# Modulation halves in four column quarters of the array, their halves added on GpSimd, their columns turned one stage later

## The reference, cut to what matters

```python
mod = silu(c) @ w_mod + b_mod        # c: 1024 values; w_mod: 1024 x 6144
shift1, scale1, gate1, shift2, scale2, gate2 = split(mod, 6)
h = rmsnorm(x, norm1_g) * (1 + scale1) + shift1
```

## Time and profile before

| what | value |
|---|---|
| median of 3 runs | 1730.06 us (1729.62 to 1731.22) |
| the profiled execution, its time | 1734.61 us |
| its span, first to last instruction | 1732.9 us |
| PE busy | 1720.6 us, 99% |
| DVE busy | 1145.7 us, 66% |
| ACT busy | 861.3 us, 50% |
| POOL busy | 231.0 us, 13% |
| chain that ended last | PE 91%, DVE 4%, DMA 2% |

### The profile page before, as it was taken

The page is one execution under the profiler, slowest core; times in us unless marked ns, Lnnn a source line. Parts: engine busy times, 40 slices in busy tenths (PEclk is TensorE's granted clock), DMA queues, the critical chain, the costliest instruction groups (busy, mean ns, idle before and its releaser), DMA issues.

```text
span 1732.9 us, 31049 instructions
## 1 busy us (share of the span) xinstructions
PE 1720.6 (99%) x12693; PEld 1579.1 (91%) x12693; DVE 1145.7 (66%) x1815; ACT 861.3 (50%) x1412; POOL 231.0 (13%) x291
## 2 busy tenths in 40 slices
PE   9999999999999999999999999999999999999999
PEld 9998798999899879998799998999877888979999
DVE  5774658786667566754677777666665747765553
ACT  5444354674444435443544754454436446555543
POOL 2000042221000000000132212000012515210000
PEclk9999999999999999999999999999999999999999
DMA  8676577445657657765676445777535434466653
GB/s 277 220 246 216 180 244 233 153 144 189 204 192 255 222 171 250 255 209 194 209 234 217 134 160 170 248 238 243 177 118 172 103 93 131 146 194 195 195 189 104
DMA packets 257518, 334.71 MB, mean 193 GB/s; under 512 B 15210, under 2 KB 217168, under 8 KB 257376
## 3 DMA queue, kind: packets, MB, share of 16 engines
q1 hardware_dynamic: 251312, 317.42, 56.4%
q0 software_dynamic: 6064, 15.31, 2.7%
HBM read 327.45 MB, written 1.05 MB: 190 GB/s over the span
## 4 chain that ended last, share of the span: by engine, by line
PE 91%; DVE 4%; DMA 2%; ACT 1%; issue 1%; POOL 0%; SPq 0%; POOLq 0%; DVEq 0%; ACTq 0%
PE bank L757 19%; PE bank L760 19%; PE bank L758 19%; PE bank L801 7%; PE bank L802 7%; PE bank L799 7%; DVE wlo L2013 2%; PE bank L923 1%; ACT whi L1571 1%; DMA mtmp<-mtmp 1%; PE bank L773 1%; PE bank L1049 1%; PE bank L883 1%; PE bank L777 1%; PE bank L781 1%
## 5 line engine op out<-in xcount | busy, mean ns | idle before, releaser
L2013 DVE TENSOR_TENSOR wlo<-raw,whi 128x1024 fp32r<-128x1024 f32 x549 | 669.8, 1228 | 335.3 <-ACT whi L1571 331.2
L1571 ACT ACTIVATE whi<-raw 128x1024 fp32r<-128x1024 f32 x549 | 572.1, 1051 | 405.8 <-PE bank L802 217.3
L757 PE MATMUL bank<-XTh,whi 128*128 128x256 f32 x1984 | 555.6, 280 | 0.0
L760 PE MATMUL bank<-XTh,wlo 128*128 128x256 f32 x1984 | 551.6, 278 | 0.5 <-DVE wlo L2013 0.5
L758 PE MATMUL bank<-XTl,whi 128*128 128x256 f32 x1984 | 551.0, 278 | 0.0
L760 PEld LDWEIGHTS bank<-XTh,wlo 128*128 128x128 f32 x1984 | 374.6, 189 | 1.5 <-DVE wlo L2013 1.4
L757 PEld LDWEIGHTS bank<-XTh,whi 128*128 128x128 f32 x1984 | 372.8, 188 | 2.3
L758 PEld LDWEIGHTS bank<-XTl,whi 128*128 128x128 f32 x1984 | 372.9, 188 | 0.0
L757 PE MATMUL bank<-HCh,whi 128*128 128x256 f32 (+2 forms) x864 | 244.3, 283 | 0.0
L758 PE MATMUL bank<-HCl,whi 128*128 128x256 f32 (+2 forms) x864 | 242.2, 280 | 0.0
L760 PE MATMUL bank<-HCh,wlo 128*128 128x256 f32 (+2 forms) x864 | 242.1, 280 | 0.0
(11 more groups left out here) (370 smaller groups left out, 2367.4 us busy)
## 6 DMA issues: line engine op xcount, KB each, us to landing
raw<-in_ffn_w_dram SPq DMA_DIRECT2D x131, 1024.0 KB, 5.2
raw<-in_w_in_dram SPq DMA_DIRECT2D x76, 1024.0 KB, 5.2
raw<-in_w_mod_dram SPq DMA_DIRECT2D x24, 1024.0 KB, 5.1
raw<-in_w_branch_dram SPq DMA_DIRECT2D x16, 1024.0 KB, 5.0
raw<-in_w_out_dram SPq DMA_DIRECT2D x12, 1024.0 KB, 5.0
raw<-in_w_ffn_gate_dram SPq DMA_DIRECT2D x11, 1024.0 KB, 5.1
raw<-in_w_ffn_up_dram SPq DMA_DIRECT2D x11, 1024.0 KB, 5.1
raw<-in_w_ffn_down_dram SPq DMA_DIRECT2D x8, 1024.0 KB, 5.0
```

Source lines behind the costliest of these rows:

```text
L757: e.matmul(o, hi[:, k, w0:w0 + nc_], xh, start=first and k == 0, stop=False)
L760: m = e.matmul(o, lo[:, k, w0:w0 + nc_], xh, start=False, stop=last and k == nk - 1)
L1571: e.activation(hi_part(n), raw_part(n), ACTF.Copy).then_inc(WHI.did(n), 1)
L2013: e.tensor_tensor(lo_part(n), raw_part(n), hi_part(n).bitcast(F32), ALU.subtract).then_inc(WLO.did(n), 1)
```

## The change

A half is now four matmuls with 32 columns of weights each, one for each block of rows, and each goes to its own 32 partitions of the bank, that is to its own column quarter of the array. The silu values lie in a row of 46, zeros behind them, so that each matmul takes 32 of them of which the first two are the ones wanted. What the other 30 columns yield is not read. The four blocks are not summed in the bank any more. The whole bank is copied to SBUF; the second half goes to a buffer of its own (one of `SUMS`), and GpSimd adds the two (`mod_rows`). Four transposes of 128 x 128 turn the sum, and DVE reduces the four quarters into the columns (`mod_turned`). L919 and `cmb` are gone. The columns of group 1 are made in the next feed-forward part, those of group 2 in the mixer in place of one `settle`, those of groups 7 and 11 where they were. In group 11 the sum of squares stands between the halves instead of inside the first.

```diff
-        csil = sb(ctx, "csil", [128, 8, 2])
+        csil = sb(ctx, "csil", [128, 46])
...
-        cmb = sb(ctx, "cmb", [4, 2])
-        sb(ctx, "gap0", [128, 40])
+        sb(ctx, "gap0", [128, 12])
...
+        def mod_rows_of(g, h):
+            if h == 0 or g == 11:
+                return spare
+            return SUMS[{1: 1, 2: 2, 7: 3}[g]][0]
...
             def modulation_half(g, h, first, last, b):
                 c = w.take_whole()
                 if first:
                     empty(b)
                     q.wait_ge(AMD, ("silu", 1))
-                    if h:
-                        q.wait_ge(AMD, ("row", g, 0))
-                        q.wait_ge(TAB, "cmb")
-                        e.matmul(bank[b][0:2, :], cmb[0:2, :], spare[0:2, :], start=True, stop=False)
                 chunk_here(q, c)
                 for k in range(4):
-                    kk = 4 * h + k
-                    m = e.matmul(bank[b][0:2, :], csil[:, kk, :], raw_whole(c)[:, k, :], start=kk == 0, stop=last and k == 3)
-                    if between and k == 1:
-                        between()
+                    m = e.matmul(bank[b][32 * k:32 * k + 32, :], csil[:, 8 * h + 2 * k:8 * h + 2 * k + 32], raw_whole(c)[:, k, :], start=first, stop=last)
...
             def mod_columns(g, b):
                 q.wait_ge(AMD, ("row", g, 1))
-                q.wait_ge(TAB, "cmb")
+                if g != 11:
+                    q.wait_ge(PLN, ("rows", g))
                 empty(b)
                 for j in range(4):
-                    e.matmul(bank[b][:, 2 * j:2 * j + 2], spare[0:2, j * 128:(j + 1) * 128], cmb[0:2, :], start=True, stop=True)
-                settle(b).then_inc(MOD.did(("columns", g)), 1)
+                    m = e.transpose(bank[b][:, j * 128:(j + 1) * 128], spare[:, j * 128:(j + 1) * 128], ident)
+                m.then_inc(MOD.did(("columns", g)), 1)
...
# tensor: layernorm
-                    if h:
-                        mod_columns(g, row_bank(j))
-                    elif j % 3:
+                    if j % 3:
                         empty(2)
                         settle(2)
# tensor: mixer, behind V
-                empty(3)
-                settle(3)
+                if l:
+                    mod_columns(2, 3)
+                else:
+                    empty(3)
+                    settle(3)
# tensor: second
-                modulation_half(11, 0, True, False, 3, add_squares)
+                modulation_half(11, 0, True, False, 3)
+                add_squares()
                 modulation_half(11, 1, False, True, 3)
# tensor: second feed-forward part of the first layer
+                at = ffn_mods(2 * l + 1)
+                if l == 0:
+                    at[0] = lambda: mod_columns(1, 7)
...
# scalar
-                e.activation(spare[0:2, :], bank[b][0:2, :], ACTF.Copy).then_inc(AMD.did(("row", g, h)), 1)
+                e.activation(mod_rows_of(g, h)[:, :], bank[b][:, :], ACTF.Copy).then_inc(AMD.did(("row", g, h)), 1)
...
# vector
+            def mod_turned(g, b):
+                q.wait_ge(MOD, ("columns", g))
+                parts_of = bank[b][:, :].rearrange("p (a j r) -> p a r j", a=4, j=4)
+                e.tensor_reduce(modc[:, 4 * g:4 * g + 4, :], parts_of[:, :, 0:2, :], AX.X, ALU.add).then_inc(DMD.did(g), 1)
...
# gpsimd
+            def mod_rows(g):
+                q.wait_ge(AMD, ("row", g, 1))
+                e.tensor_tensor(spare[:, :], spare[:, :], mod_rows_of(g, 1)[:, :], ALU.add).then_inc(PLN.did(("rows", g)), 1)
...
             def second():
                 for t in range(2):
                     unit_rows(0, t, 6 + t)
+                mod_rows(7)
                 first_block_gone(q)
...
             for l in range(2):
                 layernorm(3 * l)
+                if l:
+                    mod_rows(2)
                 mixer(l)
                 layernorm(3 * l + 1)
+                if l == 0:
+                    mod_rows(1)
```

More of the change, by code:

```diff
@@ L36 @@
 C_COS, C_SIN, C_FIRST = 384, 640, 896
-C_COSG, C_SING, C_PERMG, C_SCAN, C_GM, C_IN, C_NEG, C_CMB, C_ALL = (
-    896, 1152, 1408, 1536, 2304, 2560, 2816, 3072, 3074)
+C_COSG, C_SING, C_PERMG, C_SCAN, C_GM, C_IN, C_NEG, C_ALL = (
+    896, 1152, 1408, 1536, 2304, 2560, 2816, 3072)
 R_GB, R_DG, R_C, R_CC, R_N1, R_N2, R_BM, R_BA, R_GN, R_NQ, R_NK, R_ALL = (
@@ L578, in lo_part, with csil_of @@
             return wlo[n % 4][:, at:at + a * b].rearrange("p (k c) -> p k c", k=a)
+        def csil_of(k, m):
+            return csil[:, 2 * k + m:2 * k + m + 1]
+        def mod_rows_of(g, h):
+            if h == 0 or g == 11:
+                return spare
+            return SUMS[{1: 1, 2: 2, 7: 3}[g]][0]
         def raw_whole(c):
@@ L908, in modulation, with modulation_half @@
                 emptied[b] = ((DMD, g),)
-            def modulation_half(g, h, first, last, b, between=None):
+            def modulation_half(g, h, first, last, b):
                 c = w.take_whole()
@@ L1557, in tensor @@
                 layernorm(3 * l + 1)
-                ffn_up(2 * l + 1, xt, x_ready(3 * l + 2), ffn_mods(2 * l + 1))
+                at = ffn_mods(2 * l + 1)
+                if l == 0:
+                    at[0] = lambda: mod_columns(1, 7)
+                ffn_up(2 * l + 1, xt, x_ready(3 * l + 2), at)
                 ffn_down(2 * l + 1, context() if l else None)
@@ L1583, in mod_row @@
                 q.wait_ge(MOD, ("mod", g, h))
-                if g in ROW_BEFORE:
-                    q.wait_ge(MOD, ("columns", ROW_BEFORE[g]))
-                e.activation(spare[0:2, :], bank[b][0:2, :], ACTF.Copy).then_inc(AMD.did(("row", g, h)), 1)
+                if h == 0 or g == 11:
+                    if g in ROW_BEFORE:
+                        q.wait_ge(MOD, ("columns", ROW_BEFORE[g]))
+                e.activation(mod_rows_of(g, h)[:, :], bank[b][:, :], ACTF.Copy).then_inc(AMD.did(("row", g, h)), 1)
             def ffn_up(i, at):
@@ L1612, in silu_c @@
                 q.wait_ge(AMD, "cols")
+                q.wait_ge(PST, "sel")
+                pairs = csil[:, 0:16].rearrange("p (k m) -> p k m", m=2)
                 for j, r in enumerate((R_C, R_CC)):
-                    e.activation(csil[:, :, j], cols[:, r:r + 8], ACTF.Silu).then_inc(AMD.did(("silu", j)), 1)
+                    e.activation(pairs[:, :, j], cols[:, r:r + 8], ACTF.Silu).then_inc(AMD.did(("silu", j)), 1)
             def ffn_mods(i):
@@ L2021, in sum_up @@
                     q.wait_ge(MOD, ("columns", BEFORE[g]))
+                if (g, h) == (3, 0):
+                    q.wait_ge(PLN, ("rows", 1))
                 for k in (2 * step, 2 * step + 1):
@@ L2025, in sum_up @@
                         if kk == 0:
-                            e.tensor_scalar(acc[:, :], raw_whole(c)[:, k, :], csil[:, kk, m:m + 1], None, ALU.mult).then_inc(
+                            e.tensor_scalar(acc[:, :], raw_whole(c)[:, k, :], csil_of(kk, m), None, ALU.mult).then_inc(
                                 DMD.did(("sum", g, m, kk), ("whole", c), ("sums", g)), 1)
@@ L2029, in sum_up @@
                             q.wait_ge(DMD, ("sum", g, m, kk - 1))
-                            e.scalar_tensor_tensor(acc[:, :], raw_whole(c)[:, k, :], csil[:, kk, m:m + 1], acc[:, :], ALU.mult, ALU.add).then_inc(
+                            e.scalar_tensor_tensor(acc[:, :], raw_whole(c)[:, k, :], csil_of(kk, m), acc[:, :], ALU.mult, ALU.add).then_inc(
                                 DMD.did(("sum", g, m, kk), ("whole", c), ("sums", g)), 1)
@@ L2117, in layernorm @@
                 w.take_whole()
-                g, h = NORMS[j]
                 if turn:
@@ L2135, in mixer @@
                 w.more(3)
+                if l:
+                    mod_turned(2, 3)
                 def stats_v(t):
@@ L2156, in times_cos @@
                     q.wait_ge(AMX, ("qk", l, n))
+                    q.wait_ge(TAB, "csa")
                     e.scalar_tensor_tensor(dst[:, j, :], mtmp[tm[l].slot["s", n]][:, :], scale, cos, ALU.mult, ALU.mult).then_inc(
@@ L2360, in between @@
                     if calls[0] == 1:
-                        mod_columns(7, 3)
+                        mod_turned(7, 3)
                     if calls[0] == 2:
@@ L2622, in last_columns @@
                 def last_columns():
-                    mod_columns(11, 3)
+                    mod_turned(11, 3)
                     q.wait_ge(DMD, 11)
@@ L2650, in vector @@
                 layernorm(3 * l + 1, (2, 6)[l])
-                ffn_up(2 * l + 1, 0.5, ffn_mods(2 * l + 1))
+                at = ffn_mods(2 * l + 1)
+                if l == 0:
+                    at[0] = lambda: mod_turned(1, 7)
+                ffn_up(2 * l + 1, 0.5, at)
                 w.pass_b(NF, 4, context() if l else None)
@@ L2825, in gpsimd @@
             load_rows()
+            e.memset(csil[:, :], 0.0).then_inc(PST.did(), 1)
             e.memset(sel[:, :], 0.0).then_inc(PST.did("sel0"), 1)
```

10 lines of the change are left out of this document (2 added, 8 removed).

## The result

The changed kernel takes 1755.7 us (median of 1746.91, 1755.51, 1755.97 and 1759.23) beside 1730.6 us of the kernel before on the same chip. The ratio is 1.0132, 95% interval 1.0091 to 1.0174: slower by some 23 us. The forecast was 1735.3, the range ended at 1739.5. The sign was right, the size was not.

What follows compares the result with a forecast made beforehand. PE, busy 1720.6 of 1732.9 us, was taken as the bound, but DVE's x at the norms. Gains 2.9, less 1.5 sixth norm, 4.2 and 1.6 clock, 0.9 group 11, gave 5.3 us longer: median 1735.3, range 1727.5 to 1739.5.

Steps and rivals of the forecast that it cites:

- The half in four quarters: Each modulation half: four column quarters work at once, so it takes 0.9 us, 2.6 us shorter.
- PE waits for DVE's x at the norms: First five norms: PE idles from the half's end to DVE's first half of x, 2.6 us at the second norm.
- The gain that the sum took at the second norm: Second norm: without L919 and the columns, work restarts at 453.27 instead of 454.89, gain 1.6 us, net 1.1.
- the adds of groups 1 and 2 ... cost 0, but for 0.1 us where the add slows DVE: GpSimd's adds of groups 1 and 2: due ten us and more before their columns, so cost 0 but for 0.1 us.
- The clock: Clock falls after idle stretches: 4.2 us at three of five norms (bounds 0 and 7), 1.6 behind the sixth.
- The sixth norm's wait: Behind the sixth norm: group 7's columns wait for POOL's add of 1.6 us, a loss of 1.5 (0.9 to 2.8).
- Group 11: Last group: columns gain 0.6 us; a second clock fall less the shorter half's gain, minus 0.9 (+0.5 to -1.7).
- The gain of 2.9 us: Sum of the gains at the first five norms and group 11's columns: 0.1 + 1.1 + 1.1 + 0.6 us.
- The clock holds: Rival: the clock does not fall at the five norms; 1731.1 us, chance 0.27.
- nothing measurable: Rival: halves lie in DVE's gaps, add short, no new clock falls; 2.0 us faster, 1728.1, chance 0.08.
- GpSimd's add is long: Rival: the long add costs 2.8 us and the clock falls at all five norms; 1740.4 us, chance 0.08.
- the spared PE time comes back: Rival: `raw` buffers freed 2.6 us earlier let loads land and be split earlier; 1722 us, chance 0.10.

Runs made afterwards that it cites:

- a_late_open: a_place with GpSimd's sums of groups 1 and 2 moved away from the norms, halves still short; 1.0035 of the kernel before, 1740.2 us.
- b_short: The kernel before with one of the four matmuls of each modulation half kept at the six norms; 1.0036 of the kernel before, 1740.5 us.
- a_late: a_place_filled with GpSimd's sums of groups 1 and 2 moved away from the norms; 0.9993 of the kernel before, 1734.9 us.
- a_place: The changed kernel with csil moved behind sv2, so that HCh and its neighbours have their old addresses; 1.0075 of the kernel before, 1748.1 us.
- a_place_filled: a_place with the halves' matmuls at the six norms issued four times over; 1.0011 of the kernel before, 1735.4 us.
- a_addfirst: The changed kernel with GpSimd's sum of group 7 ahead of its two unit powers; 1.0117 of the kernel before, 1752.6 us.
- a_settle: The changed kernel with one identity transpose added behind the four transposes of group 11's columns; 1.0109 of the kernel before, 1753.3 us.
- a_small: The changed kernel with four two-column matmuls and one identity transpose added behind group 11's column transposes; 1.0101 of the kernel before, 1753.4 us.
- b_shift: The kernel before with only addresses changed: HCh moved by 128 bytes, X and all behind it by 32; 1.0198 of the kernel before, 1767.5 us.
- b_hc128: The kernel before with HCh, HCl and their neighbours 128 bytes higher, X in place; 1.0023 of the kernel before, 1738.2 us.

## Why the prediction was wrong

**The half in four quarters: right.** 0.9 us said, 1.06 measured. Four records start 6 to 7 ns apart, and 433 ns behind them four more; starts and ends of the eight records rise together.

**PE waits for DVE's x at the norms: right.** 2.6 us of idle time said, 2.48 measured. The gain that the sum took at the second norm, 1.6 us, did not come: L779 starts 6.20 us behind the half (458.46 - 452.26); before it was 6.56 behind L919, 0.4 in place of 1.6. With the sum moved it does come: in a_late_open L779 starts 5.11 us behind the half (453.90 - 448.79), a gain of 1.45.

**The step "the adds of groups 1 and 2 ... cost 0, but for 0.1 us where the add slows DVE": failed.** I had looked at when the sums are due, not at what runs beside them. Each lay beside DVE's last write of x and made it 1.755 us instead of 0.75, on the very path that PE waits for, which also prolonged the idle time. Moving both gave 7 us with the short halves (1.0075 to 1.0035), and 3 us, not clear of noise, with the filled ones (1.0011 to 0.9993). At the second norm the sum took 1.41 us and ended at 456.88, the DVE write beside it at 457.42, 1.0 us late. Why the one slows the other is not shown.

**The clock: the mechanism right, the term too small.** The term rested on one fall: in the kernel before PE idled 2.33 us before group 11, and the clock was 0.50 in the next 3.30 us. The sum had 4.2 us at the norms (three of five, 1.4 each), 1.6 behind the sixth and part of 0.9 at the end. Four of five fell (32 of 35 over all traces with short halves), and the second, the sixth and the last for 6.7 us, not 3.3. At the five norms that is 16.6 us at half clock, 8.3 us at most by the prediction's own price. The runs price it higher: b_short has short halves at 6 us in the kernel before, filling them gives 7 (a_late_open to a_late) to 11 us (a_place to a_place_filled). The upper bound of 7 was taken with one low stretch at each norm; two in a row did not occur to me.

**The sixth norm's wait: right.** The sum took 1.42 us (1.6 said), the product behind it came 3.19 - 2.04 = 1.15 us later (1.5 said). In the trace of a_addfirst, moving it ahead of the powers only changed which wait ends last; its time can't be told from either forecast.

**Group 11: about right.** The sum had 0.6 gained by the columns and 0.9 lost before them. From the first half to the product behind the columns it was 1551.85 - 1533.51 = 18.34 us and is now 1567.86 - 1549.12 = 18.74, a loss of 0.4 for 0.3. PE comes to h2 earlier, waits 2.92 us for DVE and goes on at half clock:

```profile
1533.51 1.88 PE L923 MATMUL bank<-raw,csil 128*2 128x512 f32 x4
1551.85 0.37 PE L757 MATMUL bank<-HCh,whi 128*128 128x256 f32 x1
```

```profile
1549.12 1.06 PE L924 MATMUL bank<-raw,csil 128*32 128x512 f32 x8
1557.36 5.04 PE L779 MATMUL bank<-HCh,whi 128*128 128x256 f32 x16 [2.92 <-DVE KNT L2631]
1567.86 0.36 PE L763 MATMUL bank<-HCh,whi 128*128 128x256 f32 x1
```

**What the sum did not have: the addresses.** The line of the diff that makes csil [128, 46] I priced at nothing. It moves HCh by 128 bytes and with it the streams that read HCh and HCl to the slow pace. By the count of distances that is 8.3 us; giving the old addresses back gave 10 us (1.0132 to 1.0075), which is the least certain of the steps: a_settle and a_small, the changed kernel but for one and five small instructions, came to 1.0109 and 1.0101. Alone in the kernel before it costs 4 us, since there most of the last stage stays fast. Addresses, sums and filling, 10 + 7 + 7, add up to 24 us. That is no check of the parts, since the steps lead from 1.0132 to 0.9993 one behind the other; in another order the sums have 3 and the filling 11. The gain of 2.9 us that I took is, at 0.9993 (0.9977 to 1.0010), neither shown nor excluded.

**Rivals.** "The clock holds", "nothing measurable", "GpSimd's add is long" (1.42 us measured, 2.9 in that rival) and "the spared PE time comes back" are out. The last had it that earlier buffers would help; the norms are set by DVE, as argued.

**Open:** why an address and four transposes decide a stream's pace together, and what the low stretch at 1330 us hangs on, which the short halves do not cause. That the third norm alone kept its clock was this execution's: it fell in the six other traces with short halves.

## What to carry to other kernels

Work that fills a wait is not free to remove: here TensorE idled some 2.5 us at a norm with a short half (1.6 at two in b_short), and 32 of 35 such norms were followed by 3.4 or 6.8 us at half clock, so shorten such work only if something else moves in. Price a small GpSimd operation by what VectorE does beside it (1.4 us of sum made a VectorE write 1.0 us longer), not by its due time. And when a tensor in the middle of memory changes size, keep the addresses of what lies behind it, or time that shift alone first (34 us in b_shift, 4 in b_hc128).

## What was not expected of the hardware

- A stream of 256-column matmuls without a gap, at clock 1.00, has two paces, 113.3 and 117.7 ns. It keeps one for hundreds of matmuls and changes at interruptions, and with the addresses: 32 bytes on X and 128 on HCh cost 34 us, with distances scattered around 118.3 ns in b_shift. The record of a matmul is 276 ns long at the fast pace and 279 at the slow one, the weights take 187 to 188 at either:

```profile
L757 PE MATMUL bank<-HCh,whi x207: 276/276/277, 1579.8 to 1649.9; 128*128 128x256 f32 x104
```

```profile
L763 PE MATMUL bank<-HCh,whi x199: 279/279/279, 1580.0 to 1649.9; 128*128 128x256 f32 x199
```

- One program draws its pace anew in some streams at each execution: two traces of the kernel before have 2681 and 2035 slow distances, 2.8 us apart. How much of its range over all runs here, 1728.9 to 1743.5 us, comes from that is not shown.
- Four matmuls on four column quarters run at the same time: their 8 records of 0.6 us each are done in 1.06 us.
- A GpSimd sum of 128x512 takes 1.42 us by itself, and made a VectorE operation beside it 1.0 us longer (1.755 for 0.75).
